# FFN down tiles of a two-layer decoder step, multiplied in pairs by seven block products in place of eight

## The reference

```python
def conv_ffn(x, prev, w_up, conv_w, conv_b, w_down):
    u, state = causal_dwconv(x @ w_up, conv_w, conv_b, prev)     # width 3, 6144 channels
    return (jax.nn.gelu(u[..., :D_FF]) * u[..., D_FF:]) @ w_down, state   # D_FF = 3072, D_MODEL = 1024

h = layer_norm(ALPHA * x + mix, ln_mg, ln_mb)
f, ffn_state = conv_ffn(h, ffn_prev, w_up, conv_w, conv_b, w_down)
h = layer_norm(ALPHA * h + f, ln_fg, ln_fb)
```

## Time and profile before

| what | value |
|---|---|
| median of 3 runs | 1601.13 us (1599.08 to 1601.28) |
| span of the profiled execution | 1598.8 us |
| TensorE matmuls | busy 98%, 12506 |
| VectorE, ScalarE, GpSimd | busy 63%, 45%, 20% |
| matmuls of L2098 | 77.0% of the chain that ended last |
| chunk splits | 223, mean 1057 ns (ScalarE) and 1231 ns (VectorE) |

### The profile page before, as it was taken

The page is one execution under the profiler, slowest core; times in us unless marked ns, Lnnn a source line. Parts: engine busy times, 40 slices in busy tenths (PEclk is TensorE's granted clock), DMA queues, the critical chain, the costliest instruction groups (busy, mean ns, idle before and its releaser), DMA issues.

```text
span 1598.8 us, 31456 instructions
## 1 busy us (share of the span) xinstructions
PE 1561.7 (98%) x12506; PEld 1526.9 (96%) x12506; DVE 1009.9 (63%) x1644; ACT 721.5 (45%) x1321; POOL 322.7 (20%) x742
## 2 busy tenths in 40 slices
PE   8999899988999999999999999999999999999999
PEld 8999787868999999999999999999999999999999
DVE  3346788874887445535567787868873455355684
ACT  4445677863444324314334537744443333144352
POOL 4702344420154012102210000002530121022000
PEclk9999999998999999999999999999999999999999
DMA  7746000053222222222232222242222222222322
GB/s 271 146 103 225 1 1 1 18 180 98 78 82 91 93 80 93 86 100 80 84 106 87 80 80 80 92 135 67 92 81 93 88 86 93 82 91 93 104 67 96
DMA packets 42635, 148.01 MB, mean 93 GB/s; under 512 B 6432, under 2 KB 8752, under 8 KB 42176
## 3 DMA queue, kind: packets, MB, share of 16 engines
q1 hardware_dynamic: 36864, 125.58, 24.4%
q0 software_dynamic: 5632, 20.48, 3.7%
HBM read 140.57 MB, written 9.10 MB: 94 GB/s over the span
## 4 chain that ended last, share of the span: by engine, by line
PE 87%; DVE 7%; ACT 3%; issue 2%; DMA 0%; POOL 0%; ACTq 0%; DVEq 0%
PE PS L2098 77%; PE PS L2262 2%; PE PS L2149 1%; PE PS L2150 1%; PE PS L2224 1%; ACT ARENA L867 1%; DVE SMALL L1399 1%; PE PS L2397 1%; DVE LO L491 1%; DVE PTSL L1239 1%; PE PS L2215 1%; DVE X L1705 1%; PE PS L2216 1%; DVE ARENA L1788 0%; ACT HI L485 0%
## 5 line engine op out<-in xcount | busy, mean ns | idle before, releaser
L2098 PE MATMUL PS<-XH,HI 128*128 128x272 f32 (+1 forms) x1936 | 406.5, 291 | 9.4 <-DVE XL L1239 8.6
L2098 PE MATMUL PS<-XH,LO 128*128 128x272 f32 (+1 forms) x1936 | 402.9, 289 | 0.0
L2098 PE MATMUL PS<-XL,HI 128*128 128x272 f32 (+1 forms) x1936 | 402.3, 288 | 0.0
L485 ACT ACTIVATE HI<-RAW 128x1024 fp32r<-128x1024 f32 x223 | 235.3, 1057 | 255.1 <-PE PS L2098 227.9
L491 DVE TENSOR_TENSOR LO<-RAW,HI 128x1024 fp32r<-128x1024 f32 x223 | 274.4, 1231 | 104.0 <-ACT HI L485 94.4
L2098 PEld LDWEIGHTS PS<-XH,HI 128*128 128x128 f32 x1936 | 306.9, 189 | 11.0 <-DVE LO L491 8.7
L2098 PE MATMUL PS<-GH,HI 128*128 128x272 f32 (+1 forms) x1504 | 313.7, 290 | 0.9 <-DVE LO L491 0.6
L2098 PE MATMUL PS<-GH,LO 128*128 128x272 f32 (+1 forms) x1504 | 311.1, 288 | 0.0
L2098 PE MATMUL PS<-GL,HI 128*128 128x272 f32 (+1 forms) x1504 | 310.5, 288 | 0.0
L2098 PEld LDWEIGHTS PS<-XL,HI 128*128 128x128 f32 x1936 | 305.9, 189 | 0.1
L2098 PEld LDWEIGHTS PS<-XH,LO 128*128 128x128 f32 x1936 | 304.7, 189 | 0.0
(11 more groups left out here) (384 smaller groups left out, 1900.1 us busy)
## 6 DMA issues: line engine op xcount, KB each, us to landing
RAW<-in_w_stream SPq DMA_DIRECT2D x223, 512.0 KB, 3.3
ARENA<-in_cache_cmp POOLq DMA_DIRECT2D x32, 128.0 KB, 3.2
out_win_old<-in_win_copy POOLq DMA_DIRECT2D x1, 4064.0 KB, 17.3
...
ARENA<-in_cache_win POOLq DMA_DIRECT2D x4, 512.0 KB, 5.3
...
```

The costliest lines, as they stand in the source:

```text
L485: nc.scalar.activation(HI[:, s * CH:(s + 1) * CH], RAW[:, (c % RAWS) * CH:(c % RAWS + 1) * CH], ACT.Copy).then_inc(hi_ready, 1)
L2098: ins = mm(PS[0:rows, b + h, 0:width], w[:, 0:rows], cols(part, h), start=first and len(parts) == 2 and n == 0, stop=last and len(parts) == 1)
```

## The change

In the first two thirds of each layer (CROSSED) the down tiles are done in pairs q (two pairs in each half d of a third, so d, q = 0, 1 cover the 8 tiles). The two output tiles of a pair, the two k tiles of each of 4 k pairs j, and the two column halves make 2 x 2 blocks. Seven block products with sums of operands take the place of eight (Winograd's form of Strassen's scheme). A product is 4 j x 3 = 12 matmuls into one bank. With U0, U1 the even and odd k blocks of the upper output tile and L0, L1 of the lower, E0, E1 and O0, O1 the column halves of the even and odd k tile:

- weight sums S1 = L0 + L1, S2 = S1 - U0, S3 = U0 - L0, S4 = U1 - S2; operand sums T1 = E1 - E0, T2 = O1 - T1, T3 = O1 - E1, T4 = T2 - O0
- p1 = U0 E0, p2 = U1 O0, p3 = S4 O1, p4 = L1 T4, p5 = S1 T1, p6 = S2 T2, p7 = S3 T3

GpSimd makes the weight sums (s1 to s4, 128 x 512 each) and the operand sums (272 columns), and some of the additions into X (x_add). ScalarE and VectorE split 7 pieces for two pairs in place of 4 chunks: "first" (U, for p1 and p2), "main" (S2 and S4, for p6 and p3), both for each pair, "sums" (S1 of both pairs, p5), "lower" (S3 and L1, p7 and p4). The order of the 14 products of a half is STEPS. VectorE, and ScalarE for p1, take each product from PSUM in parts of 272 columns. There are two more weight buffers (MORE, slots 2 and 3), all loads are written out, the tap weights are read from PAR and no longer copied to CWS, and the layer's p is loaded later. On ScalarE the eight biases of X move from the down tiles of the first third to its up tiles 12 to 15, and GeLU 7 goes ahead of the taking of tile 15; on VectorE product 7 goes ahead of the chunk split.

```diff
+CROSSED = (0, 1)
+STEPS = (("p1", 0), ("p1", 1), ("p2", 0), ("p2", 1), ("p3", 0), ("p3", 1), ("p5", 0), ("p5", 1),
+         ("p6", 0), ("p6", 1), ("p7", 0), ("p4", 0), ("p7", 1), ("p4", 1))
...
+            for c in LOAD_ORDER[RAWS:]:
+                if LOAD_AFTER[c] is not None:
+                    sp.wait_ge(lo_ready, LOAD_AFTER[c] + 1)
...
+                def operand_sums(t, j):
+
+                    done = 3 * (4 * crossed_before(layer, t) + j)
+                    at = lambda i: TF[:, j * TRIO + i * HALF:j * TRIO + (i + 1) * HALF]
+                    pool.wait_ge(prod_done, PROD0[layer] + 8 * t + 2 * j + 2)
+                    g.tensor_tensor(at(0), PR_ODD[:, HALF:TOK], PR_EVEN[:, HALF:2 * HALF], ALU.subtract).then_inc(t_sum, 1)
+                    g.tensor_tensor(at(1), PR_ODD[:, HALF:TOK], PR_EVEN[:, 2 * HALF:3 * HALF], ALU.subtract).then_inc(t_sum, 1)
+                    pool.wait_ge(t_sum, done + 1)
+                    g.tensor_tensor(at(2), at(0), PR_ODD[:, 0:HALF], ALU.subtract).then_inc(t_sum, 1)
...
+                def s1(t, d, q):
+                    upper, lower = rows(t, d, q)
+                    landed(pool, PIECE[product_piece(layer, t, d, "p7", q)][1])
...
+                    g.tensor_tensor(SUMS[:, q * BLOCK:(q + 1) * BLOCK].rearrange("p (k c) -> p k c", k=4), lower[:, 0], lower[:, 1],
+                                    ALU.add).then_inc(s1_summed, 1)
...
+                def crossed_down(t, d):
+
+                    for q in range(2):
+                        x_add(t, d, q, 0, 0, FIRST_SUM, ("p1", "p2"))
+                    if d == 0:
+                        s1(t, 1, 0)
+                        s3(t, 1, 0)
+                    x_add(t, d, 0, 0, 1, SECOND_SUM, ("p6",))
+                    x_add(t, d, 1, 0, 1, SECOND_SUM, ("p6",))
+                    if d == 0:
+                        s2(t, 1, 0)
+                        s4(t, 1, 0)
+                    x_add(t, d, 0, 1, 1, SECOND_SUM, ("p7",))
+                    x_add(t, d, 0, 1, 0, FIRST_SUM, ("p4",))
+                    if d == 0:
+                        s1(t, 1, 1)
+                        s3(t, 1, 1)
+                        s2(t, 1, 1)
+                        s4(t, 1, 1)
+                    x_add(t, d, 1, 1, 1, SECOND_SUM, ("p7",))
+                    x_add(t, d, 1, 1, 0, FIRST_SUM, ("p4",))
+
                 for t in range(3):
                     for n in range(16):
...
+                        first_tap(t, n)
+                        if t not in CROSSED:
+                            continue
+                        if n % 4 == 2:
+                            second_less_first(t, n // 4)
+                        elif n and n % 4 == 0:
+                            operand_sums(t, n // 4 - 1)
+                        if n == 12:
+                            s1(t, 0, 0)
+                            s3(t, 0, 0)
+                        elif n == 13:
+                            s2(t, 0, 0)
+                            s4(t, 0, 0)
+                            s1(t, 0, 1)
+                        elif n == 14:
+                            s3(t, 0, 1)
+                            s2(t, 0, 1)
+                            s4(t, 0, 1)
...
+                def first_product(t, d, q):
+                    o = product_item(layer, t, d, "p1", q)
+                    act.wait_ge(tile_done, o + 1)
+                    act.wait_ge(x_added, x_added_by(layer, t, d - 1, q, 1, 0))
+                    s.activation(FIRST_SUM[q], product_bank(o), ACT.Copy).then_inc(act_took, 1)
...
+                        w = slice(at, at + P)
+                        xh, xl = operand(step, j)
+                        mm(product_bank(o), HI[:, w], xh, start=j == 0, stop=False)
+                        mm(product_bank(o), HI[:, w], xl, start=False, stop=False)
+                        ins = mm(product_bank(o), LO[:, w], xh, start=False, stop=j == 3)
...
+                    if t in CROSSED:
+                        one_product(t, 0, "p1", 0)
+                        one_product(t, 0, "p1", 1)
+                        for js in (range(3), range(3, 4)):
+                            one_product(t, 0, "p2", 0, js)
+                            one_product(t, 0, "p2", 1, js)
+                            one_product(t, 0, "p3", 0, js)
+                        for step, q in STEPS[5:]:
+                            one_product(t, 0, step, q)
+                        for step, q in STEPS:
+                            one_product(t, 1, step, q)
+                        continue
```

More of the change, by code:

```diff
@@ new lines, in plan @@
+        plain(f"proj{layer}", 8, lambda n: "act", lambda n: [n // 4], lambda n: (n + 1) % 2)
+        plain(f"gate{layer}", 8, lambda n: "act", one, lambda n: (1, 0, 2, 1, 0, 1, 0, 1)[n])
+    used_up = [sum(1 for u in last_user if u <= o) for o in range(len(taker))]
+    in_a_row = [next((c for c, u in enumerate(last_user) if u > o), len(piece)) for o in range(len(taker))]
+    before = [sorted({x for b in bank[o] for x in [max((x for x in range(o) if b in bank[x]), default=None)] if x is not None})
+              for o in range(len(bank))]
@@ L97 @@
+    return (first_piece, first_item, first_chunk, taker, pair, last_user, used_up, in_a_row, before, bank, piece, load_order, load_after,
+            slot_of, turn_of, where, piece_at)
+(C0, O0, CHUNK0, TAKER, PAIR, LAST_USER, USED_UP, IN_A_ROW, BEFORE, BANK, PIECE, LOAD_ORDER, LOAD_AFTER,
+ SLOT_OF, TURN_OF, WHERE, PIECE_AT) = plan()
+N_CHUNKS, N_PIECES = len(SLOT_OF), len(PIECE)
 RAWS, SLOTS, AHEAD = 2, 4, 3
@@ new lines, in s4, with x_add @@
+                def s4(t, d, q):
+                    upper, _ = rows(t, d, q)
+                    pool.wait_ge(s2_summed, pairs_before(t, d, q) + 1)
+                    g.tensor_tensor(upper[:, 1], upper[:, 1], upper[:, 0], ALU.subtract).then_inc(s4_summed, 1)
+                def x_add(t, d, q, row, h, what, after):
+                    for step in after:
+                        wait_taken(pool, product_item(layer, t, d, step, q))
+                    at = x_half(4 * d + 2 * q + row, h)
+                    g.tensor_tensor(at, at, what[q], ALU.add).then_inc(x_added, 1)
@@ L2101, in products, with tile @@
                     ins.then_inc(done, 1)
-            def tile(o, c, ks, xh, xl, x0, rows=P, t=None, each=None, width=HALF):
-                ready(o, c, t)
+            def tile(o, c, ks, xh, xl, x0, rows=P, each=None, width=HALF):
+                ready(o, c)
                 for n, k in enumerate(ks):
```

527 lines of the change are left out of this document (369 added, 158 removed).

## The result

| | median, us | span of the profiled execution | granted clock, mean |
|---|---|---|---|
| before | 1600.74 (1599.08 to 1601.28) | 1598.8 | 0.997 |
| after | 1673.66 (1670.51 to 1676.82) | 1671.9 | 0.978 |

The ratio is 1.0455 [1.044, 1.047]: slower, as forecast, but by 73 us and not by 31. The time lies above the range (1585 to 1655).

What follows compares the result with a forecast made beforehand. TensorE's unbroken matmuls were taken to bound the kernel. A third: -6.03 + 6.8 + 6.9 = +7.7, four of them +30.7, so 1631.8 us against the median of 1601.1; range 1585 to 1655, the forecast's own 1604 to 1655.

Steps and rivals of the forecast that it cites:

- Matmuls: Crossed thirds: 84 matmuls a pair in place of 96, 192 fewer at 125.6 ns, saving 24.1 us, 6.03 a third.
- At nothing: Dropped copies of tap weights, unrolled loads, later load of p and biases moved ahead on ScalarE were costed at nothing.
- the catch-up: Start of a layer, VectorE full: GpSimd's sums lengthen it by some 4 us, but it ends before tile 12.
- Price of a sum: GpSimd's two-input sum: 1.21 us at 512 columns, 0.80 at 272, of which 0.88 and 0.47 shut VectorE out.
- Hand-over: From up to down tiles: tile 15's first tap 6.7 us late, no slack left, stall 6.8 us a third.
- Laid one after the other: Up tiles 12 to 15: VectorE and GpSimd instructions by turns take 24.8 us; the matmuls allow 18.1.
- Between the halves: Second half of a third: "main" piece 5.2 us late, "sums" piece 1.7 later than needed; together 6.9 a third.
- the late ring slot: Second half's last chunk reuses the "lower 1" buffer: VectorE until 17.3, load 3.3, so 20.8 us.
- rival 4: TensorE itself slows in stalls of 5 us, by a lower granted clock; given no time or chance of its own.
- Rival 1: GpSimd and VectorE share the port more finely, or the second input costs little: faster, 1577 to 1593; chance 0.26.
- Rival 2: The sum cancels at a price near 1.0, with 6.0 us of stalls a third: 1601; chance 0.06.
- Rival 3: Dearer sums on GpSimd: at the upper price +15.5 us a third, 1663; chance 0.08 beyond 1655.

## Why the prediction was wrong in size

*Matmuls, -24.1:* right. The count is 12314, and at full clock their pace is that of before. *At nothing:* right for what the run without crossing shows (1.0003), wrong for the catch-up (below).

*Price of a sum:* the middle value was right for the length (1.29 measured, 1.21 taken; 0.77 for 272 columns, 0.80 taken). The split of it was not: less is fixed (0.20, not 0.33) and more shuts VectorE out (1.10, not 0.88). The estimate from the Trainium skill (GPSIMD Engine Reference, "Elementwise — side-by-side cycle accounting"), 1.37, was as far off on the other side.

*Hand-over, predicted 6.8 a third:* the mechanism was right, the wait that ends the pause was not the one named. "Laid one after the other" gave 24.8 between the first taps of tiles 12 and 15. Measured in the second third: 671.31 to 697.29, 26.0, and a pause of 7.6 in place of 6.8 in both layers. The larger shut-out (0.22 more for each of eight sums) would give 1.8, so it is enough for the 1.2 more. GpSimd's first taps of tiles 12 and 15 there, and between them VectorE's low part of product 6:

```profile
671.31 0.81 POOL L815 TENSOR_SCALAR ARENA<-ARENA,PAR 128x560 f32<-128x560 f32 x1
...
695.04 1.78 DVE L1504 TENSOR_TENSOR GL<-ARENA,GH 128x544 fp32r<-128x544 f32 x1
...
697.29 0.81 POOL L815 TENSOR_SCALAR ARENA<-ARENA,PAR 128x560 f32<-128x560 f32 x1
```

TensorE goes on at 696.87, when that low part is done, and before GpSimd touches tile 15. So the whole pause is the one at the fourth operand pair, of which the prediction said that a part would show there, and product 7's low part, for which it reckoned the 6.8, delayed nothing. In the first third that one was done at 541.71, and TensorE, slowed behind the pause, reached it at about 543.0; where the extra matmuls kept the clock up, it did cost 0.67. Both low parts stand behind the same two engines' turns, which is why the size came out near: in part luck.

**The first step that failed** is "it ends before tile 12", of the catch-up. In the first third the tap of tile 12 is still shut out by VectorE and late (508.72 in the first row), while ScalarE takes tile 14 from TensorE at 516.68 (second row):

```profile
508.72 2.11 POOL L815 TENSOR_SCALAR ARENA<-ARENA,PAR 128x560 f32<-128x560 f32 x1
...
516.68 0.69 ACT L1249 ACTIVATE ARENA<-PS,SMALL 128x512 f32<-128x512 f32 x1 [0.51 <-PE PS L2429]
```

Tile 12's tap is done at 510.80, 5.9 before tile 14 is taken; in the second third it is done at 672.08, 10.05 before (682.13). So the chain starts 4.2 late, and the pause is 4.2 longer (11.78 against 7.62); in layer 1 2.5 longer. With the 2.5 among the up tiles of each first third, what I costed at nothing in the catch-up cost 11.7. The 2.5 isn't the weight sums' (it is 2.5 with 4 or 256 columns and with memsets too) and it isn't there without crossed thirds. Where VectorE's splits are longer, 1.40 each, it is 3.2. So it comes from the work added ahead of tile 12 to a full VectorE; which part of it, stays open.

*Between the halves, predicted 6.9:* 5.1 measured, which is the 5.2 of the "main" piece. (Its terms add up to 34.2 and not 33.9, which would make it 5.6.) The four last sums of this wait (562.70 to 568.81) and ScalarE and VectorE behind them are in the order that was laid out. The 1.7 more for the "sums" piece did not show: in the kernel after no further pause follows in that half. The matmuls at half clock behind the pause gave that piece more time; where the extra matmuls kept the clock up, 0.58 of wait appeared.

**The second step that failed** is a queue not read through: at the end of a third the split that waits for a load stands ahead of the evacuations. The prediction had the late ring slot and the 3.3 us load for one piece, but followed them only into the pause between the halves. It cost 9.6 of pauses, and 11.9 with what hung on them by the run that moved it.

**The third, and largest,** is rival 4, given nothing. The earlier trace rows show clock 1.00 in a stretch with 0.6 us of pauses in 35. That is no evidence on pauses of 5 us, which my own sum put eight times into the stretch. Nor was it "the stretch with the longest pauses before". Just ahead of layer 0's FFN, TensorE had pauses of 2.0, 1.5 and 0.8 us within 8 us, and there the kernel before shows the half clock, in the same view:

```profile
360.00:365.00 5.00, 2.78 (x64) 2.56 (x67) 3.46 (x11) 3.04 (x6) 0.00 (x0) 0.82 0.32 107
365.00:370.00 5.00, 2.76 (x52) 2.00 (x44) 3.13 (x11) 0.76 (x3) 0.14 (x1) 0.50 0.34 128
370.00:375.00 5.00, 5.00 (x29) 5.00 (x29) 0.05 (x1) 0.00 (x0) 0.92 (x2) 0.66 0.55 189
```

29 matmuls in the last 5 us, where the next 5 have 42: the price of 1.6 us could be read before the change. Some 20 of the 73.1 lie here, and without crossed thirds the clock was 0.999 over the kernel. What keeping it up is worth is less (4.5 measured, with the pauses filled in part), since matmuls that come sooner meet the next wait sooner.

Together: pauses 73.3 for 54.8 predicted, longer busy time, mostly the clock, 23.9 for 0, which is the 42.4 between +30.7 and +73.1. Rival 1 is refuted in both its halves: a port shared more finely by the splits of 2.32, a cheap second input by the 1.29. Rival 2's point, a price near 1.0, lies on the other side of the 1.29 measured. Rival 3 was nearer in time (1663), but for another reason than it gave: the sums were not much dearer than taken, the rest was in the three steps above.
